# Hybrid decoder block on one core: order of the first two experts' products and of four experts' weight loads, and three small moves

## The chip, the cores and the metric

The kernel runs on one core of one Trainium2 chip. The metric is the device time of one execution in microseconds (us), as the median of several runs. The engines are TensorE (PE, with its weight loads as PEld), VectorE (DVE), ScalarE (ACT), GpSimd (POOL) and SyncE (SP), which issues nearly all DMAs.

## The reference

One layer on 256 tokens of width 1024: a mixer part (an S5 state-space branch and an attention branch with indexer-chosen keys), and then a mixture of 32 experts, 4 for each token:

```
x = x + W_out( sigmoid(g_ssm) * P_ssm(y_ssm) + sigmoid(g_att) * P_att(y_att) )
h = rms_norm(x, norm2_g)
gates = softmax over the top 4 of (h @ w_router + b_router)
for e in range(32):
    z = h @ w_moe_in[e] + b_moe_in[e]                 # 1024 -> 2048
    zg, zl = min(z[:, ::2], 7), clip(z[:, 1::2], -7, 7)
    act = zg * sigmoid(1.702 * zg) * (zl + 1)
    out += gates[:, e:e+1] * (act @ w_moe_out[e] + b_moe_out[e])   # 1024 -> 1024
x = rms_norm(x + out, norm_f_g)
```

Everything is float32. The weights of the experts are 32 times 12.6 MB and are read from HBM once.

## The kernel before

**Memory.** The tensor `mem` holds 24 slots of 1 MB (128 partitions of 2048 floats). An expert has 12: eight with the weights of its input products, four with those of its output products. Even experts live in slots 0 to 11, odd ones in 12 to 23. Two neighbouring slots are a chunk, so an expert is four input chunks (n = 0 to 3) and two output chunks (n = 4, 5). During the mixer part the slots hold the mixer's data, and experts 0 and 1 are loaded into them one after the other as they come free (`load_first`, line 333).

**The loads.** SP issues DMAs in the order of its program, and before each it waits until the chunk that it overwrites has been used: `chunk_used` counts chunks of which TensorE has finished the matmuls. So a load of expert e + 2 waits for the same chunk of expert e. `load_first_pieces` (line 400) loads expert 2 in smaller pieces, each behind a mark `first_used` that TensorE sets inside a chunk. Then come the chunks of expert 3, and after that pairs of experts up to 31. The first experts come in loads of 2 MB, the middle ones of 4 MB, the last expert's last slots in pieces.

**An expert on TensorE** (`body`, line 1474), for expert j:
- input products (line 1496): 8 slots, 8 matmul records each, into PSUM banks 0 and 1; after the first slot (the fourth for expert 0) the input bias (line 1509), and for expert 1 also the output biases of all experts (line 1514);
- `scatter(j - 1)` (line 1469): adds the previous expert's output to the token sums in banks 4 to 7;
- `gather(j + 1)` (line 1452): picks the next expert's token rows into bank 3;
- four transposes of the activation into bank 0 (line 1522), two of the gates (line 1526) into bank 1, and `gather_t(j + 1)` (line 1460), which transposes the gathered rows;
- output products (line 1536) into bank 2.

DVE clamps and multiplies the activation (lines 1104 to 1110), makes the gate matrices, and copies the gathered rows and the transposed gates (line 1115, semaphore `gated_t_ok`) out of PSUM. ACT makes the sigmoid (line 667), copies the gathered rows (`h_tok`, line 648), the transposed activation (`act_t`, line 670) and the output sums (`y_tok`, line 678, in the same place as `h_tok`). The next expert's input products wait for `h_sel_ok` and `gated_t_ok`.

**The last expert** (`last_body`, line 1543) works in two halves of columns. ACT's part of it is `halves_of_act` (line 652).

**In the mixer part** TensorE transposes the first attention probabilities (`turn_prob(0)`, line 1297) and then makes the gate projection A3 (line 1337, two column blocks m).

Of the kernel before, what the change touches and what calls it, by code (L numbers as in the profile page):

```python
# [23 lines left out]
D = 1024  # L24
# [51 lines left out]
def build(nc, io, out):  # L76
# [3 lines left out]
    with ExitStack() as ctx:  # L80
# [100 lines left out]

        def act_tile(k):

            return act_t[:, 2 * (k // 4) + k % 2, k // 2 % 2, :]

# [138 lines left out]
        def _(sp):  # L324
# [68 lines left out]
            def one_pass(c, first, most_tokens=None):  # L393
# [6 lines left out]
                def load_first_pieces():  # L400

                    def piece(n, first_col, end, arrived):
                        sp.dma_start(place_of(0, n)[:, first_col:end], expert_part(2, n)[:, first_col:end]).then_inc(
                            arrived, 16)

                    sp.wait_ge(first_used, 1)
                    piece(0, 0, SW // 2, pieces_in)
                    sp.wait_ge(first_used, 2)
                    piece(0, SW // 2, SW, pieces_in)
                    sp.wait_ge(chunk_used, 1)  # L410
                    piece(0, SW, 2 * SW, moe_in[0][0])
# [70 lines left out]
        def _(ac):  # L482
# [162 lines left out]
            def one_pass(c, first, most_tokens=None):  # L645
                def gathered_rows(j):
                    ac.wait_ge(gathered, j + 1)
                    ac.activation(h_tok, ps[:, 3, :], ACT.Copy).then_inc(h_tok_ok, 1)  # L648

                turned = ps[:, 0, :].rearrange("p (j q s) -> p j q s", q=2, s=SLOTS)  # L650

                def halves_of_act(j):

                    ac.wait_ge(first_z_gate, c + 1)
                    ac.activation(sig[:, 0:256], gate_z[:, 0:256], ACT.Sigmoid, scale=ALPHA).then_inc(first_sig_ok, 1)
                    ac.wait_ge(z_gate, j + 1)
# [7 lines left out]
                def whole_act(j):  # L664

                    ac.wait_ge(z_gate, j + 1)
                    ac.activation(sig, gate_z, ACT.Sigmoid, scale=ALPHA).then_inc(sig_ok, 1)  # L667
                    gathered_rows(j + 1)
                    ac.wait_ge(act_trans, j + 1)
                    ac.activation(act_t, turned, ACT.Copy).then_inc(act_t_ok, 1)  # L670

                def body(j, tail=False):
                    if tail:
                        halves_of_act(j)
                    else:
                        whole_act(j)
                    ac.wait_ge(chunk_used, j * NT + NT)
                    ac.activation(y_tok, ps[:, 2, :], ACT.Copy).then_inc(y_tok_ok, 1)  # L678
                gathered_rows(first)
                body(first)  # L680
                if most_tokens:
                    most_tokens()
                with ac.Fori(1, NE - 1) as e:
# [21 lines left out]
        def _(ve):  # L705
# [334 lines left out]
            def one_pass(c, first, most_tokens=None):  # L1040
# [58 lines left out]

                def body(j, e):  # L1100
                    choose(e + 1)
                    ve.wait_ge(chunk_used, j * NT + NT_IN)
                    z = ps[:, 0:2, :].rearrange("p b (c g) -> p g (b c)", g=2)
# [18 lines left out]
                if isinstance(c, int):  # L1122
                    gates_out()
                body(first, 0)
                if most_tokens:
                    most_tokens()
                with ve.Fori(1, NE - 1) as e:
                    body(e + first, e)
# [18 lines left out]
        def _(pe):  # L1147
# [298 lines left out]
            def one_pass(c, first, most_tokens=None):  # L1446
# [26 lines left out]

                def body(j, odd, pair=None, big=None, head=False, out_bias=False):

                    def arrived(n):

                        if big is None:
                            pe.wait_ge(moe_in[odd][n], pair)
                        elif n % RUN == 0:  # L1480
                            pe.wait_ge(big_in[odd][n // RUN], big)

                    def weights(k):

                        return mem[:, (12 * odd + k) * SW:(12 * odd + k + 1) * SW]

# [3 lines left out]
                    for k in range(KD):  # L1490
                        if k % CH == 0:
                            arrived(k // CH)
                        w = weights(k)
# [22 lines left out]
                    if not head:  # L1516
                        scatter(j - 1)
                    gather(j + 1)
# [4 lines left out]
                    i.then_inc(act_trans, 1)  # L1523
                    pe.wait_ge(gated_ok, j + 1)
# [3 lines left out]
                    gather_t(j + 1)  # L1528

                    pe.wait_ge(act_t_ok, j + 1)  # L1530
                    for k in range(KF):
                        if k % (2 * CH) == 0:
                            arrived(NT_IN + k // (2 * CH))
                        w = weights(KD + k // 2)[:, (k % 2) * D:(k % 2) * D + D]
                        for q in range(2):
                            i = pe.matmul(ps[64 * q:64 * q + SLOTS, 2, :], act_tile(k), w[:, 512 * q:512 * q + 512],  # L1536
                                          start=(k == 0), stop=(k == KF - 1))
                        if head and isinstance(c, int) and k == 1:
                            i.then_inc(first_used, 1)
                        if k % (2 * CH) == 2 * CH - 1:  # L1540
                            i.then_inc(chunk_used, 1)

                def last_body(j):
# [84 lines left out]
                begun = 16 * SMALL * c  # L1628
                body(first, 0, pair=begun + 16, head=True)
                body(first + 1, 1, pair=begun + 16, out_bias=isinstance(c, int))  # L1630
                if most_tokens:
                    pe.wait_ge(pieces_in, 64)
                    most_tokens()
# [155 lines left out]
```

## Time and profile before

| what | value |
|---|---|
| median of 3 runs | 1137.95 us (1137.3 to 1138.54) |
| profiled execution | 1136.45 us, of which the span is 1134.6 us |
| PE busy | 1102.4 us, 97% of the span |
| DVE busy | 342.1 us, 30% |
| ACT busy | 154.7 us, 14% |
| granted TensorE clock, mean | 0.999 |
| DMA | 437.28 MB, mean 385 GB/s |

Busy times are sums over an engine's instructions with overlaps counted once. Around the span lie 1.85 us of the profiled execution's own time. Times below count from the span's start.

### The profile page before, as it was taken

The page shows a single profiled execution, that of the slowest core. Times are in us where ns is not written, and L with a number is a line of the kernel's source. Part 1 is how long each engine was busy: PE and PEld are TensorE (multiplying, and loading weights), DVE is VectorE, ACT ScalarE, POOL GpSimd, SP SyncE. Part 2 cuts the span into 40 slices and gives each one's busy share as a digit, 9 for nine tenths or more (in the row PEclk, how much of TensorE's full clock was granted, in tenths as well). Part 3 has the DMA queues.
Part 4 walks back from the last instruction along what each step waited for, and adds up shares of the span by engine and source line. Part 5 has one row for each costly group of instructions (what it writes and reads, how often), then busy time and mean ns, then how long its engine had stood idle before and what let it go on. Part 6 is the DMA issues. An engine that isn't in the chain of part 4 may idle for free.

```text
span 1134.6 us, 13388 instructions
## 1 busy us (share of the span) xinstructions
PE 1102.4 (97%) x5570; PEld 482.9 (43%) x5570; DVE 342.1 (30%) x761; ACT 154.7 (14%) x319; POOL 0.7 (0%) x8
## 2 busy tenths in 40 slices
PE   9999999999999999999999999999999999999996
PEld 8888888833333333333333333333333333333332
DVE  7999993132121111111111111111111111111112
ACT  2410361220100000100000000000000000000002
POOL 0000000000000000000000000000000000000000
PEclk9999999999999999999999999999999999999999
DMA  8444577799999999999999999999999999999996
GB/s 341 140 151 143 197 290 313 325 362 401 427 427 436 429 435 429 430 434 430 432 434 429 432 433 431 434 431 430 434 430 432 433 430 432 433 424 427 427 425 261
DMA packets 26095, 437.28 MB, mean 385 GB/s; under 512 B 3152, under 2 KB 3408, under 8 KB 6096
## 3 DMA queue, kind: packets, MB, share of 16 engines
q1 hardware_dynamic: 25632, 436.05, 91.2%
q10 hardware_dynamic: 432, 0.79, 0.2%
q8 instruction: 23, 0.38, 0.1%
q14 instruction: 8, 0.07, 0.0%
HBM read 434.99 MB, written 1.05 MB: 384 GB/s over the span
## 4 chain that ended last, share of the span: by engine, by line
PE 63%; DMA 22%; DVE 6%; issue 1%; ACT 0%; another core or an unknown queue 0%; SPq 0%; DVEq 0%; ACTq 0%
PE ps L1496 29%; DMA mem<-in_w_moe 22%; PE ps L1536 13%; PE ps L1469 4%; PE ps L1452 4%; PE ps L1398 2%; PE ps L1509 2%; DVE mem L714 2%; PE ps L1572 1%; PE ps L1169 1%; PE ps L1356 1%; PE ps L1460 1%; PE ps L1522 1%; DVE mem L901 1%; DVE xs L714 1%
## 5 line engine op out<-in xcount | busy, mean ns | idle before, releaser
L1496 PE MATMUL ps<-mem,late 128*64 128x512 f32 x1984 | 440.9, 595 | 17.0 <-DMA mem<-in_w_moe 17.0
L1496 PEld LDWEIGHTS ps<-mem,late 128*64 128x64 f32 x1984 | 138.2, 137 | 313.6 <-issue 283.0
L1104 DVE TENSOR_SCALAR late<-ps 128x512 f32<-128x512 f32 x31 | 21.4, 692 | 658.6 <-PE ps L1496 658.6
L1536 PE MATMUL ps<-mem,late 128*64 128x512 f32 x992 | 219.7, 595 | 0.0
L1169 PE MATMUL ps<-mem 128*128 128x256 f32 x608 | 135.3, 381 | 0.2 <-issue 0.2
L1536 PEld LDWEIGHTS ps<-mem,late 128*64 128x64 f32 x992 | 68.5, 137 | 129.1 <-issue 124.1
L1169 PEld LDWEIGHTS ps<-mem 128*128 128x128 f32 x608 | 114.4, 190 | 19.2 <-issue 4.0
L667 ACT ACTIVATE late<-late 128x512 f32<-128x512 f32 x31 | 19.5, 630 | 491.0 <-DVE late L1104 491.0
L1469 PE MATMUL ps<-late 64*128 64x512 f32 x256 | 63.6, 615 | 0.9 <-ACT late L678 0.9
L1452 PE MATMUL ps<-xs,late 128*64 128x512 f32 x256 | 61.9, 604 | 0.2 <-DVE late L714 0.2
L714 DVE TENSOR_TENSOR mem<-mem 128x1024 f32<-128x1024 f32 (+8 forms) x88 | 60.0, 723 | 1.3
L678 ACT ACTIVATE late<-ps 128x512 f32<-128x512 f32 x32 | 19.1, 597 | 227.2 <-PE ps L1536 223.5
L714 DVE TENSOR_TENSOR late<-late 128x128 f32<-128x128 f32 (+3 forms) x99 | 38.5, 417 | 7.1 <-ACT late L643 1.3
L1469 PEld LDWEIGHTS ps<-late 64*128 64x128 f32 x256 | 22.1, 186 | 41.9 <-issue 41.9
L1509 PE MATMUL ps<-bias_rows,late 32*64 32x512 f32 x248 | 33.7, 613 | 0.0
L1452 PEld LDWEIGHTS ps<-xs,late 128*64 128x64 f32 x256 | 15.7, 136 | 42.2 <-issue 41.5
L714 DVE TENSOR_TENSOR late<-ps,vec 128x512 f32<-128x512 f32 x32 | 22.1, 692 | 35.5 <-PE ps L1460 35.5
L714 DVE TENSOR_TENSOR mem<-ps,mem 128x1024 f32<-128x1024 f32 (+2 forms) x30 | 25.9, 899 | 17.2 <-PE ps L1356 9.2
L648 ACT ACTIVATE late<-ps 128x512 f32<-128x512 f32 x32 | 19.2, 599 | 73.9 <-PE ps L1452 73.9
L1398 PE MATMUL ps<-mem 128*128 128x256 f32 x128 | 28.9, 380 | 0.0
L1398 PEld LDWEIGHTS ps<-mem 128*128 128x128 f32 x128 | 23.8, 190 | 3.4 <-issue 0.4
L714 DVE TENSOR_TENSOR late<-table,late 128x128 f32<-128x128 f32 x96 | 24.6, 283 | 0.2
(185 smaller groups left out, 527.0 us busy)
## 6 DMA issues: line engine op xcount, KB each, us to landing
mem<-in_w_moe SPq DMA_DIRECT2D x66, 4096.0 KB, 41.3
mem<-in_w_moe SPq DMA_DIRECT2D x54, 2048.0 KB, 16.0
mem<-in_w_mix SPq DMA_DIRECT2D x26, 1024.0 KB, 6.0
mem<-in_w_moe SPq DMA_DIRECT2D x10, 1024.0 KB, 22.8
mem<-in_w_moe SPq DMA_DIRECT2D x4, 512.0 KB, 18.0
out<-xs SPq DMA_DIRECT2D x2, 512.0 KB, 2.8
mem<-in_x_t ACTq DMA_DIRECT2D x3, 256.0 KB, 4.9
mem<-mem SPq DMA_DIRECT2D x12, 64.0 KB, 2.0
```

Source lines behind the costliest of these rows:

```text
L648: ac.activation(h_tok, ps[:, 3, :], ACT.Copy).then_inc(h_tok_ok, 1)
L667: ac.activation(sig, gate_z, ACT.Sigmoid, scale=ALPHA).then_inc(sig_ok, 1)
L678: ac.activation(y_tok, ps[:, 2, :], ACT.Copy).then_inc(y_tok_ok, 1)
L714: return ve.tensor_tensor(out_, a, b, op)
L1104: ve.tensor_scalar(gate_z, z[:, 0], LIMIT, None, ALU.min).then_inc(z_gate, 1)
L1169: i = pe.matmul(b[:, m * T:m * T + T], slot[:, k, first_m + m, :], src[:, k, :], start=(k == 0), stop=(k == kt - 1))
L1398: i = pe.matmul(b[:, 0:T], wide(f"W{m // 2}")[:, k, m % 2, :], mixed[:, k, :], start=(k == 0), stop=(k == KD - 1))
L1452: i = pe.matmul(ps[64 * q:64 * q + SLOTS, 3, :], one_hot[:, t, :], xs[:, t, 512 * q:512 * q + 512], start=(t == 0), stop=(t == TT - 1))
L1469: i = pe.matmul(ps[:, 4 + 2 * t + q, :], gated_t[r, t * P:t * P + P], y_tok[r, :], start=False, stop=False, skip_group_check=True)
L1496: i = pe.matmul(ps[r, n // 2, :], h_sel[:, k % 4, k // 4, :], w[:, 512 * n:512 * n + 512], start=(k == 0), stop=(k == KD - 1))
L1509: pe.matmul(ps[r, n // 2, :], chosen[g, n, :], b_in[g, :], start=False, stop=False)
L1536: i = pe.matmul(ps[64 * q:64 * q + SLOTS, 2, :], act_tile(k), w[:, 512 * q:512 * q + 512], start=(k == 0), stop=(k == KF - 1))
```

## The change

The first two experts are no longer two `body` calls. `first_pair` does the input products of expert 0, its activation, the input products of expert 1, then the output products of 0, and those of 1. The transposed activation of expert 0 goes to the place of `h_tok` meanwhile. The loads follow this order: input chunks of expert 2 in pieces of 1 MB (two new marks after k = 4 and k = 6), input chunks of expert 3, output chunks of expert 2, output chunks of expert 3. Apart from that, three moves: the block m = 0 of A3 stands ahead of `turn_prob(0)`; for expert 30 `scatter(29)` stands behind k = 3 of the input products; in the last expert ACT copies the first half of `act_t` ahead of the second half's sigmoid.

```diff
 SP, load_first_pieces
-                    sp.wait_ge(first_used, 3)
-                    piece(1, 0, SW, pieces_in)
-                    sp.wait_ge(chunk_used, 2)
-                    piece(1, SW, 2 * SW, moe_in[0][1])
-                    load_part(1, 0, 2)
-                    load_part(1, 0, 3)
-                    sp.wait_ge(first_used, 4)
-                    piece(NT_IN, 0, SW, pieces_in)
-                    sp.wait_ge(chunk_used, NT_IN + 1)
-                    piece(NT_IN, SW, 2 * SW, moe_in[0][NT_IN])
-                    load_part(1, 0, NT - 1)
+                    for n in range(1, NT_IN):
+                        sp.wait_ge(first_used, n + 2)
+                        piece(n, 0, SW, pieces_in)
+                        sp.wait_ge(chunk_used, n + 1)
+                        piece(n, SW, 2 * SW, moe_in[0][n])
+                    for n, (half, part) in enumerate([(1, n) for n in range(NT_IN)]
+                                                     + [(h, n) for h in range(2) for n in range(NT_IN, NT)]):
+                        sp.wait_ge(chunk_used, NT_IN + n + 1)
+                        sp.dma_start(place_of(half, part), expert_part(2 + half, part)).then_inc(moe_in[half][part], 16)
...
-                    load_pair(1, halves=range(1, 2))
 ACT, last expert
+                    ac.wait_ge(first_act_trans, c + 1)
+                    ac.activation(act_t[:, 0:2], turned[:, 0:2], ACT.Copy).then_inc(first_act_t_ok, 1)
                     ac.wait_ge(z_gate, j + 1)
                     ac.activation(sig[:, 256:512], gate_z[:, 256:512], ACT.Sigmoid, scale=ALPHA).then_inc(sig_ok, 1)
-                    ac.wait_ge(first_act_trans, c + 1)
-                    ac.activation(act_t[:, 0:2], turned[:, 0:2], ACT.Copy).then_inc(first_act_t_ok, 1)
 ACT, first pair
+                def first_pair():
+                    gate_of(0)
+                    gathered_rows(1)
+                    ac.wait_ge(h_trans, 2)
+                    turned_act(0, act_t_aside)
+                    gate_of(1)
+                    sums_out(NT + NT_IN)
+                    turned_act(1, act_t)
+                    gathered_rows(2)
+                    sums_out(2 * NT)
 DVE: body(1) stands ahead of the loop, and waits for 8 chunks used instead of 10
+                    body(1, 1, used=2 * NT_IN)
 PE, mixer part
-            pe.wait_ge(tables_in, 16)
-            turn_prob(0)
             chunk_arrived(pe, "A3")
             for m in range(2):
                 for k in range(KD):
...
+                if m == 0:
+                    pe.wait_ge(tables_in, 16)
+                    turn_prob(0)
 PE, experts
-                            if head and isinstance(c, int) and (k, n) in ((0, 1), (0, 3), (2, 3)):
+                            if head and isinstance(c, int) and (k, n) in ((0, 1), (0, 3), (2, 3), (4, 3), (6, 3)):
                                 i.then_inc(first_used, 1)
...
+                        if scatter_early and k == 3:
+                            scatter(j - 1)
...
+                def first_pair():
+                    into(0, 0, pair=16, head=True)
+                    gather(1)
+                    turn_act(0)
+                    turn_gated(0)
+                    gather_t(1)
+                    pe.wait_ge(act_t_ok, 1)
+                    into(1, 1, pair=16, out_bias=True)
+                    back(0, 0, pair=16, turned=act_t_aside)
+                    turn_act(1)
+                    scatter(0)
+                    turn_gated(1)
+                    gather(2)
+                    gather_t(2)
+                    back(1, 1, pair=16)
...
-                body(first + NE - 2, 0, pair=begun + 80)
+                body(first + NE - 2, 0, pair=begun + 80, scatter_early=True)
```

`into` is the part of `body` with the waits and the input products, `back` that with the output products.

## Rows read from the trace of the kernel before

**Rows 1.** The page, part 2: GB/s in 40 equal slices of the span.
```profile
GB/s 341 140 151 143 197 290 313 325 362 401 427 427 436 429 435 429 430 434 430 432 434 429 432 433 431 434 431 430 434 430 432 433 430 432 433 424 427 427 425 261
```
**Rows 2.** Window around the first experts: busy time of each engine, clock, DMA share, GB/s.
```profile
238.00:258.00 20.00, 18.60 (x94) 6.35 (x92) 4.67 (x11) 1.82 (x3) 0.00 (x0) 1.00 0.93 364
```
**Rows 3.** Timeline of PE at its first wait for weights.
```profile
761.37 7.09 PE L1496 MATMUL ps<-mem,late 128*64 128x512 f32 x32 [1.10 <-DMA mem<-in_w_moe]
```
**Rows 4.** 2 MB loads: last input chunk of expert 2, first and last of expert 3.
```profile
L398 SPq DMA_DIRECT2D mem<-in_w_moe x1: 328/328/328, 252.5 to 252.5; - x1
DMA to landing us min/median/max: 10.0/10.0/10.0
L398 SPq DMA_DIRECT2D mem<-in_w_moe x1: 328/328/328, 269.8 to 269.8; - x1
DMA to landing us min/median/max: 9.8/9.8/9.8
L398 SPq DMA_DIRECT2D mem<-in_w_moe x1: 328/328/328, 292.3 to 292.3; - x1
DMA to landing us min/median/max: 11.8/11.8/11.8
```
**Rows 5.** 2 MB loads issued in the mixer part behind an idle or short queue.
```profile
L337 SPq DMA_DIRECT2D mem<-in_w_moe x1: 328/328/328, 140.2 to 140.2; - x1
DMA to landing us min/median/max: 7.2/7.2/7.2
L337 SPq DMA_DIRECT2D mem<-in_w_moe x1: 328/328/328, 197.1 to 197.1; - x1
DMA to landing us min/median/max: 8.7/8.7/8.7
```
**Rows 6.** Timeline of PE and DVE, experts 0 and 1: start, us, what.
```profile
245.33 7.09 PE L1496 MATMUL ps<-mem,late 128*64 128x512 f32 x32
257.00 7.09 PE L1536 MATMUL ps<-mem,late 128*64 128x512 f32 x32
257.71 0.41 DVE L1115 COPY late<-ps 128x256 f32<-128x256 f32 x1
263.92 1.89 PE L1496 MATMUL ps<-mem,late 128*64 128x512 f32 x8
279.99 1.99 PE L1469 MATMUL ps<-late 64*128 64x512 f32 x8
285.13 7.09 PE L1536 MATMUL ps<-mem,late 128*64 128x512 f32 x32
```
**Rows 7.** Timeline of PE and DVE, experts 30 and 31, and the last weight load.
```profile
1077.65 3.65 PE L1496 MATMUL ps<-mem,late 128*64 128x512 f32 x16 [0.65 <-DMA mem<-in_w_moe]
1082.54 3.65 PE L1496 MATMUL ps<-mem,late 128*64 128x512 f32 x16 [1.24 <-DMA mem<-in_w_moe]
1091.27 7.09 PE L1536 MATMUL ps<-mem,late 128*64 128x512 f32 x32
1117.09 1.94 PE L1592 MATMUL ps<-mem,late 128*64 128x512 f32 x8 [1.25 <-ACT late L659]
1117.14 0.42 DVE L714 TENSOR_TENSOR late<-late 128x256 f32<-128x256 f32 x1
1119.54 5.37 PE L1592 MATMUL ps<-mem,late 128*64 128x512 f32 x24
L447 SPq DMA_DIRECT2D mem<-in_w_moe x1: 4241/4241/4241, 1090.5 to 1090.5; - x1
DMA to landing us min/median/max: 32.1/32.1/32.1
```
**Rows 8.** Timeline of the mixer part: the first probabilities' transposes, a later DVE eviction, the third projection job.
```profile
155.41 1.06 PE L1297 MATMUL ps<-table,xs 128*128 128x128 f32 x8 [1.40 <-DVE xs L714]
170.34 1.28 DVE L714 TENSOR_TENSOR mem<-ps,mem 128x512 f32<-128x512 f32 x2
171.25 3.72 PE L1169 MATMUL ps<-mem 128*128 128x256 f32 x16
```

More of the change, by code:

```diff
@@ L180, in build, with act_tile @@
         gates_t = cut(3776, T)
-        def act_tile(k):
-            return act_t[:, 2 * (k // 4) + k % 2, k // 2 % 2, :]
+        act_t_aside = h_tok.rearrange("p (j q s) -> p j q s", q=2, s=SLOTS)
+        def act_tile(k, src=None):
+            return (act_t if src is None else src)[:, 2 * (k // 4) + k % 2, k // 2 % 2, :]
         def early_cut(base, n):
@@ L662, in halves_of_act, with gate_of, turned_act, sums_out @@
                     ready(ACT.Sqrt)
-                def whole_act(j):
+                def gate_of(j):
                     ac.wait_ge(z_gate, j + 1)
                     ac.activation(sig, gate_z, ACT.Sigmoid, scale=ALPHA).then_inc(sig_ok, 1)
+                def turned_act(j, dst):
+                    ac.wait_ge(act_trans, j + 1)
+                    ac.activation(dst, turned, ACT.Copy).then_inc(act_t_ok, 1)
+                def sums_out(used):
+                    ac.wait_ge(chunk_used, used)
+                    ac.activation(y_tok, ps[:, 2, :], ACT.Copy).then_inc(y_tok_ok, 1)
+                def first_pair():
[8 more added lines that the diff above has]
+                    sums_out(2 * NT)
+                def whole_act(j):
+                    gate_of(j)
                     gathered_rows(j + 1)
-                    ac.wait_ge(act_trans, j + 1)
-                    ac.activation(act_t, turned, ACT.Copy).then_inc(act_t_ok, 1)
+                    turned_act(j, act_t)
                 def body(j, tail=False):
@@ L676, in body @@
                         whole_act(j)
-                    ac.wait_ge(chunk_used, j * NT + NT)
-                    ac.activation(y_tok, ps[:, 2, :], ACT.Copy).then_inc(y_tok_ok, 1)
+                    sums_out(j * NT + NT)
                 gathered_rows(first)
-                body(first)
+                if isinstance(c, int):
+                    first_pair()
+                else:
+                    body(first)
+                    body(first + 1)
                 if most_tokens:
                     most_tokens()
-                with ac.Fori(1, NE - 1) as e:
+                with ac.Fori(2, NE - 1) as e:
                     body(e + first)
@@ L1098, in last_body, with body @@
                     ve.tensor_copy(gated_t, ps[:, 1, 0:T]).then_inc(gated_t_ok, 1)
-                def body(j, e):
+                def body(j, e, used=None):
                     choose(e + 1)
-                    ve.wait_ge(chunk_used, j * NT + NT_IN)
+                    ve.wait_ge(chunk_used, j * NT + NT_IN if used is None else used)
                     z = ps[:, 0:2, :].rearrange("p b (c g) -> p g (b c)", g=2)
@@ L1124, in one_pass @@
                 body(first, 0)
+                if isinstance(c, int):
+                    body(1, 1, used=2 * NT_IN)
+                else:
+                    body(first + 1, 1)
                 if most_tokens:
                     most_tokens()
-                with ve.Fori(1, NE - 1) as e:
+                with ve.Fori(2, NE - 1) as e:
                     body(e + first, e)
@@ L1472, in scatter, with arrived, weights, into @@
                             i.then_inc((first_sum_ok, second_sum_ok)[t], 1)
[L1474 to L1485, printed above, removed]
+                def arrived(odd, n, pair, big):
+                    if big is None:
+                        pe.wait_ge(moe_in[odd][n], pair)
+                    elif n % RUN == 0:
+                        pe.wait_ge(big_in[odd][n // RUN], big)
+                def weights(odd, k):
+                    return mem[:, (12 * odd + k) * SW:(12 * odd + k + 1) * SW]
+                def into(j, odd, pair=None, big=None, head=False, out_bias=False, scatter_early=False):
                     pe.wait_ge(h_sel_ok, j + 1)
@@ L1491, in body @@
                         if k % CH == 0:
-                            arrived(k // CH)
-                        w = weights(k)
+                            arrived(odd, k // CH, pair, big)
+                        w = weights(odd, k)
                         for n in range(4):
@@ L1515, in body, with turn_act @@
                                           start=False, stop=False, skip_group_check=True)
-                    if not head:
-                        scatter(j - 1)
-                    gather(j + 1)
+                        if scatter_early and k == 3:
+                            scatter(j - 1)
+                def turn_act(j):
                     pe.wait_ge(act_ok, j + 1)
@@ L1523, in body, with turn_gated @@
                     i.then_inc(act_trans, 1)
+                def turn_gated(j):
                     pe.wait_ge(gated_ok, j + 1)
@@ L1527, in body, with back @@
                     i.then_inc(gated_trans, 1)
-                    gather_t(j + 1)
+                def back(j, odd, pair=None, big=None, turned=None):
                     pe.wait_ge(act_t_ok, j + 1)
@@ L1532, in body @@
                         if k % (2 * CH) == 0:
-                            arrived(NT_IN + k // (2 * CH))
-                        w = weights(KD + k // 2)[:, (k % 2) * D:(k % 2) * D + D]
+                            arrived(odd, NT_IN + k // (2 * CH), pair, big)
+                        w = weights(odd, KD + k // 2)[:, (k % 2) * D:(k % 2) * D + D]
                         for q in range(2):
-                            i = pe.matmul(ps[64 * q:64 * q + SLOTS, 2, :], act_tile(k), w[:, 512 * q:512 * q + 512],
+                            i = pe.matmul(ps[64 * q:64 * q + SLOTS, 2, :], act_tile(k, turned), w[:, 512 * q:512 * q + 512],
                                           start=(k == 0), stop=(k == KF - 1))
-                        if head and isinstance(c, int) and k == 1:
-                            i.then_inc(first_used, 1)
                         if k % (2 * CH) == 2 * CH - 1:
                             i.then_inc(chunk_used, 1)
+                def body(j, odd, pair=None, big=None, head=False, scatter_early=False):
+                    into(j, odd, pair, big, head, scatter_early=scatter_early)
+                    if not head and not scatter_early:
+                        scatter(j - 1)
+                    gather(j + 1)
+                    turn_act(j)
+                    turn_gated(j)
+                    gather_t(j + 1)
+                    back(j, odd, pair, big)
+                def first_pair():
[13 more added lines that the diff above has]
+                    back(1, 1, pair=16)
                 def last_body(j):
@@ L1628, in one_pass @@
                 begun = 16 * SMALL * c
-                body(first, 0, pair=begun + 16, head=True)
-                body(first + 1, 1, pair=begun + 16, out_bias=isinstance(c, int))
+                if isinstance(c, int):
+                    first_pair()
+                else:
+                    body(first, 0, pair=begun + 16, head=True)
+                    body(first + 1, 1, pair=begun + 16)
                 if most_tokens:
-                    pe.wait_ge(pieces_in, 64)
+                    pe.wait_ge(pieces_in, 80)
                     most_tokens()
```

## The prediction

> **What bounds the kernel now.** I read the page's slices first. From about a quarter of the span on, HBM delivers close to 430 GB/s in every slice, while in the slices before it delivers less [rows 1]. PE is called busy 97%, so both have to be looked at. The window of the first experts shows where the DMA stream is not yet full: 364 GB/s in the 20 us from 238 on, in which expert 2's loads begin [rows 2]. Then I looked for the place where PE first waits for weights: 761.37 [rows 3]. Until there PE is the slower reader of weights that are long in memory, but the loads behind it queue up, and from there on every expert's time is the stream's. The end is therefore set by when the stream became full, plus the bytes that remain, plus what PE does after the last weights. In the tail, PE waits twice for input chunks of expert 30, 0.65 us and 1.24 us, and from 1082.54 on it is PE's own chain, with one gap of 1.25 us behind ACT at 1117.09 [rows 7]. The last piece lands at 1090.5 + 32.1 = 1122.6; PE needs it for its last sixth of the 5.37 us from 1119.54, so at 1119.54 + 5 x 0.89 = 1124.0. PE is only 1.4 us behind it.
>
> So three sums matter: the delay of the stream when it becomes full, PE's chain from 1082.5 on, and the slack between this chain and the last pieces.
>
> **Mixer part: A3's first block ahead of the transposes.** PE stands 1.40 us at 155.41 for the probabilities [rows 8]. A3's first block fills that gap (its 16 matmul records of the kind of the projection job's 16, which take 3.72 us), so A3 ends up to 1.4 us earlier. But the third projection job, at 171.25, needs a PSUM bank that DVE empties in the first half of the 1.28 us from 170.34, so at 170.98 [rows 8], and nothing in DVE's chain to there waits for PE's new order. So only 0.2 us is left. PE is dense after that, so the expert part starts 0.2 us earlier.
>
> **The first pair on PE.** Expert 0's input products end as now, at 245.33 + 7.09 = 252.4. Gather, activation and transposes are the same instructions in the same order, and take until 257.0 [rows 6]. Nothing is gained there: PE still waits for expert 0's activation before it does anything of expert 1. Then come expert 1's input products, and these wait for more than the output products did: `gated_t_ok`, which DVE gives at 257.71 + 0.41 = 258.12 [rows 6]. ACT's copy of the activation must be over too, which now waits for `gather_t`; it ends at about the same time. They start at 257.9 with the 0.2 us taken off. They last 279.99 - 263.92 = 16.1 us, to 274.0, and expert 0's output products 6.9 us, to 280.9. The activation of expert 1 is hidden behind these. Before the second output products 285.13 - 279.99 = 5.1 us of transposes, scatter and gather remain [rows 6], and ACT's copy of the gathered rows now has nothing under it, some 0.7 us. The second output products run from about 286.8 to 293.8, where they ended at 292.1 before. PE's pair takes 1.7 us longer, which costs nothing by itself: PE has slack until 761.
>
> **The first pair in the DMA stream.** This is the term that counts. Before, a load of expert 3's first chunk was issued at 269.8 and landed 9.8 us later, at 279.6; its last landed at 292.3 + 11.8 = 304.1. From the first to the last that is five more chunks in 24.5 us, 4.9 us each: full. Between the last input chunk of expert 2 (252.5 + 10.0 = 262.5) and 279.6 lie expert 2's output weights (4 MB) and the first of these chunks (2 MB): three times 4.9 us would be 14.7, it took 17.1, so 2.4 us are lost [rows 4].
>
> After, the next thing that SP may issue behind expert 2's input chunks is expert 3's first, and it has to wait until PE has used expert 1's first chunk. That takes 269.80 - 263.92 = 5.9 us from the start of its input products, since both bias groups lie inside it [rows 4, 6]: issue at 257.9 + 5.9 = 263.8. Expert 2's input chunks are then in: the new marks let four of them be issued 1 MB at a time and close a small hole, so that they land near 261 instead of 262.5. The stream stands idle, for some 5 us between landings, where the old order had issued an output slot as soon as PE had used it (257.0 + a quarter of 7.1, 258.8). The 1 MB gained early doesn't survive this hole. A 2 MB load into an idle queue landed in 7.2 us, into a partly busy one in 8.7 [rows 5]; I take 7.2, as this queue is empty. So the first chunk lands at 271.0, and all others follow without a hole, each 4.9 us later: the issues of expert 3's input chunks are 3.4 us apart, those of expert 2's output chunks fall at 277.5 and 280.9, and those of expert 3's output chunks at 290.3 and 293.8, when they need not land before 300.4 and 305.3, 10.1 and 11.5 us later. Seven more chunks: 271.0 + 7 x 4.9 = 305.3. Before it was 304.1. **The stream becomes 1.2 us later.** The bounds: landing in 8.7 gives +2.7; input products that could start at 257.0, with no wait for the copy, give +0.1.
>
> The Trainium skill ("DMA: Bandwidth & Descriptors", "Latency and other measured facts") speaks of some 2 us of fixed cost per DMA; with 4.9 us of transfer that is an estimate of 6.9 for the restart and 0.3 less in the sum. The trace has 7.2, and that is used.
>
> **The tail.** Expert 30: the scatter moves from behind the last input slot to behind the fourth. PE has 0.65 + 1.24 = 1.9 us of waits for DMA behind that place, and the scatter takes 1.9 us, so it just fits. But behind the input products its 1.9 us covered DVE's activation chain. Expert 0, which has no scatter there, shows what remains without it: 257.00 - 252.42 = 4.6 us, against 1091.27 - 1086.19 = 5.1 us in expert 30 [rows 6, 7]. The gain is 0.5 us and not 1.9. Expert 31: ACT's first-half copy no longer waits for DVE's second half, so the output products start at 1115.9 instead of 1117.09, 1.2 us earlier. The second half's product ends at 1117.14 + 0.42 = 1117.56 [rows 7], just when PE has done the first two output slices (1.8 us). So PE's chain could be 1.7 us shorter. The pieces limit it: the last lands at 1122.6, the 1 MB piece two before it by the stream's pace 2.4 us earlier, at 1120.2. PE would want that one at 1121.4 - 1.7 = 1119.7, so 0.5 us are lost to it, and the last piece at 1124.0 - 1.2 = 1122.8, which is just in time. **The tail gives 1.2 us** (0.5 if only one of the two takes effect, 1.7 if the pieces come earlier).
>
> **Sum.** +1.2 (stream, with the 0.2 us earlier start in it) - 1.2 (tail) = 0.0. Against the profiled execution (1136.45, span 1134.6) nothing changes; the median shown is 1.5 us above that execution, and the sum moves it from 1137.95 to 1138.0. 0.2% of the time is 2.3 us, about what a measurement of this kernel can tell from no change.
>
> **Rivals.**
> 1. *The restart is dear.* The landing takes 8.7 us or more, or into a queue whose engines start apart, and the tail's pieces are late by as much, so that the tail gives only 0.5: +2.7 - 0.5 = +2.2, 1140.2, and with any further wait ahead of expert 1's input products 1141. For it: in the first window the stream got 364 GB/s although issues were there [rows 2]. Against it: the idle-queue landing of 7.2. It decides if the first landing of expert 3 is later than 272.5. Chance 0.2.
> 2. *The stream runs evener after one long hole than after several small ones.* Between 304.1 and 1122.6 it moved 336 slots of 1 MB in 818.5 us, 2.436 us each. If the small holes of before left its 16 engines apart, and a restart from idle sets them level, at the 2.428 us of 4.86 us for a chunk it would gain 336 x 0.008 = 2.7 us; with the sum 0.0 that is 1135.3. For it: the landings of before are spread over 2.4 us of losses [rows 4]. Against it: 4.9 us from the first loads on, with no change later that rows show. It decides if the last landing minus that of expert 3's last chunk is under 816.5. Chance 0.1, and 0.05 more for a hole smaller than I think with the whole 1.7 us of the tail (0.1 - 1.7, 1136.3).
> 3. *The tail's moves do nothing*, because the last pieces set the end whatever PE does: +1.2, 1139.2. Against it: the 1.4 us of slack. Chance 0.1.
>
> The forecast holds the rest, 0.55, with its own range of 1136.7 to 1139.5.
>
> **Numbers.** Faster by over 0.2% needs most of rival 2: 0.13. Slower by over 0.2% is half of rival 1 and a little unforeseen: 0.17. The range from 1135.3 (rival 2) to 1140.8 (rival 1 with its bound) leaves out no more than 2 in 10.
>
> **What would show it.** Step by step: the first transposes of the probabilities start near 157.5; the second half of expert 0's input products starts at 245.1 instead of 245.33; expert 1's input products start near 257.9; the load behind them is issued at 263.8 and lands at 271; a window from 260 to 265 shows a DMA share under 0.4; the last chunk of expert 3 lands at 305.3; PE's gap between input and output products of expert 30 is 4.6 us; there is no gap at expert 31's first output products; the last piece lands 1.2 us later than 1122.6. The prediction is wrong if the first landing of expert 3 is far from 271, or if output products of expert 31 wait for their pieces longer than 0.5 us.

## The result, and the profile after

The changed kernel takes 1141.26 us (median of 8 runs, 1139.68 to 1142.83), the kernel before 1138.01 us (8 runs). The ratio is 1.0026, with a 95% interval of 1.0017 to 1.0035: 3.0 us slower by the ratio, 3.25 by the medians. Forecast was 1138.0, with a range to 1140.8. The ratios and counts below leave out two executions in a slower state (2319.12 us of the changed kernel with the hole filled, 1279.01 us of the kernel before with a longer wait of PE).

The executed order is as the prediction followed it. The times drift away from it step by step: the first transposes of the probabilities start at 157.69 (predicted 157.5), the second half of expert 0's input products at 245.42 (245.1), expert 1's input products at 258.48 (257.9), and the load behind them is issued at 265.7 (263.8). First come the windows around the first experts. Each row has the window, its length, the busy times of PE, PEld, DVE, ACT and POOL, and then the granted clock, the DMA share and GB/s. The second window lies in the hole of the stream, and the last four lie across the start of expert 1's input products:

```profile
238.00:258.00 20.00, 17.76 (x90) 5.93 (x86) 4.57 (x11) 1.82 (x3) 0.00 (x0) 0.99 0.93 364
262.00:266.00 4.00, 4.00 (x28) 1.14 (x22) 0.00 (x0) 0.00 (x0) 0.00 (x0) 1.00 0.00 0
258.00:259.00 1.00, 0.52 (x2) 0.33 (x4) 0.42 (x2) 0.00 (x0) 0.00 (x0) 0.50 1.03 434
259.00:260.00 1.00, 1.00 (x4) 0.27 (x2) 0.00 (x0) 0.00 (x0) 0.00 (x0) 0.50 1.03 434
260.00:261.00 1.00, 1.00 (x4) 0.27 (x2) 0.00 (x0) 0.00 (x0) 0.00 (x0) 0.50 0.47 197
261.00:262.00 1.00, 1.00 (x8) 0.21 (x8) 0.00 (x0) 0.00 (x0) 0.00 (x0) 0.92 0.14 57
```

The first window is as before, 364 GB/s [rows 2]. Then the hole is there: no byte between 262 and 266. And something that the prediction didn't have: TensorE's clock is 0.50, its lower level of 1.2 GHz, while expert 1's first slot is worked on. The timeline of PE and DVE shows what came ahead of it and what it cost:

```profile
256.56 0.60 PE L1491 MATMUL ps<-table,late 128*128 128x128 f32 x4
257.81 0.41 DVE L1141 COPY late<-ps 128x256 f32<-128x256 f32 x1
258.48 3.25 PE L1527 MATMUL ps<-mem,late 128*64 128x512 f32 x8 [1.32 <-DVE late L1141]
275.82 7.04 PE L1572 MATMUL ps<-mem,late 128*64 128x512 f32 x32
289.06 7.09 PE L1572 MATMUL ps<-mem,late 128*64 128x512 f32 x32
```

PE stands 1.32 us for the copy of the transposed gates. Ahead of that it waits 1.13 us for the activation and 0.28 us for the gate matrix, as it did before the change. The first slot's eight records take 3.25 us, where the same eight took 1.89 before [rows 6]: 1.36 us more. Then the loads, each with its time to landing: expert 2's last input chunk, expert 3's first, second and last chunk, and the last weight load of the kernel:

```profile
L405 SPq DMA_DIRECT2D mem<-in_w_moe x1: 327/327/327, 252.6 to 252.6; - x1
DMA to landing us min/median/max: 10.0/10.0/10.0
L422 SPq DMA_DIRECT2D mem<-in_w_moe x1: 327/327/327, 265.7 to 265.7; - x1
DMA to landing us min/median/max: 7.2/7.2/7.2
L422 SPq DMA_DIRECT2D mem<-in_w_moe x1: 328/328/328, 269.2 to 269.2; - x1
DMA to landing us min/median/max: 10.1/10.1/10.1
L422 SPq DMA_DIRECT2D mem<-in_w_moe x1: 328/328/328, 296.2 to 296.2; - x1
DMA to landing us min/median/max: 12.4/12.4/12.4
L447 SPq DMA_DIRECT2D mem<-in_w_moe x1: 4252/4252/4252, 1094.2 to 1094.2; - x1
DMA to landing us min/median/max: 33.4/33.4/33.4
```

Expert 3's first load is issued at 265.7 and lands in 7.2 us, at 272.9; the next lands at 279.3, and the last at 308.6, where it was 304.1 [rows 4]: 4.5 us later. The last load of the kernel lands at 1127.6 instead of 1122.6 [rows 7], 5.0 us later. The profiled execution is 4.7 us longer than that of before (1141.16 against 1136.45).

Expert 2's last input chunk lands at 252.6 + 10.0 = 262.6, where the prediction had it near 261, as its new marks were to close a small hole; before it was 262.5 [rows 4]. Nothing rested on that, since the stream then stands in either case.

In the tail, again PE:

```profile
1081.29 1.99 PE L1500 MATMUL ps<-late 64*128 64x512 f32 x8
1083.21 7.30 PE L1527 MATMUL ps<-mem,late 128*64 128x512 f32 x32
1093.35 0.66 PE L1554 MATMUL ps<-table,late 128*128 128x128 f32 x4 [1.13 <-DVE late L740]
1095.31 7.09 PE L1572 MATMUL ps<-mem,late 128*64 128x512 f32 x32
1120.24 1.94 PE L1653 MATMUL ps<-mem,late 128*64 128x512 f32 x8
1125.23 3.65 PE L1653 MATMUL ps<-mem,late 128*64 128x512 f32 x16 [0.59 <-DMA mem<-in_w_moe]
```

The scatter at 1081.29 fills the waits for DMA. From the end of expert 30's input products (1083.21 + 7.30 less the 0.07 by which a record overlaps the next, 1090.44) to its output products it is 4.9 us, against 5.1 before. PE now stands 1.13 us for DVE's activation, which the scatter used to cover; the prediction had 4.6. Expert 31's output products start with no gap, and PE then waits 0.59 us for a piece. From the last landing to the end of the last output products, it is 1.3 us (1127.6 to 1128.9) instead of 2.3 (1122.6 to 1124.9): the tail gave 1.0 us.

In the mixer part A3 fills the gap, and the time comes back at the third projection job:

```profile
154.14 3.72 PE L1365 MATMUL ps<-mem 128*128 128x256 f32 x16
171.37 3.69 PE L1199 MATMUL ps<-mem 128*128 128x256 f32 x16 [1.25 <-DVE mem L740]
```

### The profile page after: what moved, and what is told of

The parts are those of the page before. It is cut to its first block, busy times and chain, and to the rows that moved or that the text cites. A ratio compares the mean times of both kernels' runs of the same rounds, so it can differ in the third digit from the quotient of the medians.

```text
span 1139.1 us, 13377 instructions
## 1 busy us (share of the span) xinstructions
PE 1104.7 (97%) x5570; PEld 483.5 (42%) x5570; DVE 342.1 (30%) x761; ACT 154.7 (14%) x319; POOL 0.7 (0%) x8
## 4 chain that ended last, share of the span: by engine, by line
PE 62%; DMA 21%; DVE 7%; issue 1%; ACT 1%; another core or an unknown queue 0%; SPq 0%; DVEq 0%; ACTq 0%
PE ps L1527 30%; DMA mem<-in_w_moe 21%; PE ps L1572 14%; PE ps L1500 4%; PE ps L1483 4%; PE ps L1429 2%; PE ps L1540 2%; DVE mem L740 2%; PE ps L1387 1%; PE ps L1491 1%; PE ps L1554 1%; DVE xs L740 1%; DVE mem L927 1%; PE ps L1199 1%; DVE mem L942 1%
## 5 line engine op out<-in xcount | busy, mean ns | idle before, releaser
L740 DVE TENSOR_TENSOR mem<-ps,mem 128x1024 f32<-128x1024 f32 (+2 forms) x30 | 25.9, 899 | 17.1 <-PE ps L1387 9.2
L1554 PEld LDWEIGHTS ps<-table,late 128*128 128x128 f32 x124 | 13.0, 140 | 27.5 <-issue 23.5
```

Of the source, the lines that this page charges most:

```text
L740: return ve.tensor_tensor(out_, a, b, op)
```

## The experiments

All are measured beside the kernel before on the same chip. The ratio is to that kernel, and differences in us are worked out from it. "Landing" is the last landing of expert 3's weights minus the first issue for expert 2, from each profile; it takes out the up to 1.2 us by which the expert part as a whole starts earlier or later in one profile than in another (first issues from 238.4 to 239.6). It is 65.7 for before and 70.1 for the changed kernel.

| kernel | median us | ratio (95% interval) | landing |
|---|---|---|---|
| three moves alone | 1136.97 | 0.9991 (0.9982 to 1.0) | 66.0 |
| first pair alone | 1142.57 | 1.0041 (1.0027 to 1.0055) | 68.8 |
| changed, 4 matmuls in the second idle stretch | 1140.95 | 1.0025 (1.0014 to 1.0036) | 69.7 |
| changed, hole filled | 1139.19 | 1.0007 (0.9997 to 1.0016) | 68.2 |
| changed, 2 + 2 matmuls in both idle stretches | 1140.41 | 1.0019 (1.0011 to 1.0028) | 68.8 |
| changed, 2 + 2 matmuls, hole filled | 1136.92 | 0.9991 (0.9982 to 0.9999) | 66.5 |
| before, PE waits longer at expert 0 | 1139.15 | 1.001 (1.0001 to 1.0019) | 67.3 |
| before, stream stopped | 1145.77 | 1.0064 (1.005 to 1.0079) | 74.1 |
| ACT's swap alone | 1136.48 | 0.9987 (0.9978 to 0.9996) | 65.8 |
| early scatter alone | 1137.94 | 0.9996 (0.9987 to 1.0005) | 66.3 |
| A3's block alone | 1138.42 | 0.9999 (0.999 to 1.0008) | 66.2 |
| three moves, fine pieces | 1136.48 | 0.9987 (0.9978 to 0.9996) | 66.2 |

**The two halves of the change.** First the three moves without the first pair, and the first pair without the three moves.

> The kernel before with the three small moves alone (A3's first block ahead of the transposes, expert 30's scatter behind k = 3, ACT's first-half copy ahead of the second sigmoid). Theory A (the moves give what was predicted, the loss is all in the first pair): 1.2 us faster than before, gap of expert 30 between input and output products 4.6 us, no gap at expert 31's first output products. Theory B (the last pieces set the end whatever PE does, so the moves give nothing): within 0.3 us of before.

> The changed kernel without the three small moves, so the order of the first pair and its loads alone. Theory A (hole in the stream of weights, and TensorE's clock that falls in the longer idle time of PE ahead of expert 1's input products): 4 to 4.5 us slower than before; expert 3's first chunk issued near 265.7, its last landing near 308.6, a stretch of half clock near 258 to 261. Theory B (moves give nothing): the same as the changed kernel, 3.2 us slower than before.

The moves alone are 1.0 us faster (0.0 to 2.0), at the edge of what the interval resolves; the pair alone is 4.7 us slower (3.1 to 6.3). So the loss is the pair's. Theory B, which gave the moves nothing, is not borne out, though this interval alone doesn't exclude it; the swap alone, below, does. In the profile of the pair alone the clock stayed at 1.00: its landing is 68.8 and not 70.1, and that execution (1140.61) was the fastest of five; the other four had a mean clock of 0.996 or 0.997 and took 1141.75 to 1143.39. The expectation of half clock in its profile was a miss that told the most: the fall of the clock comes in most executions, not in all.

**The clock.** The changed kernel's own executions part in the same way: the five with a mean clock of 0.994 to 0.997 took 1141.16 to 1142.83 us, the three with 0.998 took 1139.68 to 1140.26. A lower clock goes with some 2 us, and 1.8 us of the loss (1139.84, the middle one of the three, against 1138.01) are there without it.

In the changed kernel, four matmuls on constants stand in PE's idle time:

```diff
                     gather_t(1)
+                    pe.wait_ge(gates_t_ok, 1)
+                    for _ in range(4):
+                        pe.matmul(ps[:, 2, 0:TB_ONE], ident, table[:, 0:TB_ONE], start=True, stop=True)
                     pe.wait_ge(act_t_ok, 1)
```

> The changed kernel with four matmuls on constants (320 columns, into a bank that nothing reads) in PE's idle time behind the transposes of expert 0. If the clock falls for that idle time and this makes the load of expert 3 late: clock at 1.00 through 250 to 270, expert 1's first slot in 1.8 us instead of 3.2, the load issued at 264.3 instead of 265.7, the last landing of expert 3 near 307.2, the median 1.4 us under the changed kernel's, its spread from run to run smaller too. If the fall of the clock has another cause: no difference.

The clock stayed up in the profile (two of seven executions still had a mean of 0.997), but the four took 2.3 us and expert 1's first slot began at 259.56. What the clock gave, the matmuls took: the time is that of the changed kernel. So two of them went behind `gather(1)`, into the other idle stretch, and two stayed:

> The changed kernel with two matmuls on constants in each of PE's two idle stretches between expert 0's input products and expert 1's (behind the gather, and behind the last transposes), so that they delay nothing: each two take 1.1 us in a stretch of 1.1 to 1.3. Four behind the transposes took 2.3 us and started expert 1 1.1 us late, as much as the clock had cost. If the fall of the clock is what idle time costs on top of the hole: clock 1.00 through 250 to 270, expert 3's first load issued at 264.3 to 264.6 (with the first load of expert 2 at 238.5), median 1.0 to 1.4 us under the changed kernel's, so 1.8 to 2.2 over before. If the clock costs nothing: 3.2 over before.

```profile
254.79 1.34 PE L1593 MATMUL ps<-table 128*128 128x320 f32 x4
257.63 1.24 PE L1598 MATMUL ps<-table 128*128 128x320 f32 x4
259.11 1.94 PE L1527 MATMUL ps<-mem,late 128*64 128x512 f32 x8 [0.24 <-DVE late L1141]
```

These are PE's rows of that kernel: the eight records take 1.94 us again, and the landing is 68.8, as in the pair alone at full clock. The time is 2.2 us over before by the ratio, with the three moves in it. That is 0.8 under the changed kernel where 1.0 to 1.4 was expected, and the two intervals overlap, so this pair of runs alone doesn't show what the clock is worth. Eight of its eleven executions had a mean clock of 0.998 or 0.999; three still had 0.997.

The other way round, the kernel before with one wait more, so that PE idles longer:

```diff
                     pe.wait_ge(act_t_ok, j + 1)
+                    if head and isinstance(c, int):
+                        pe.wait_ge(gated_t_ok, 1)
```

> The kernel before, in its own order, with one wait added: expert 0's output products wait for the copy of the transposed gates, as the change makes expert 1's input products do. PE then stands 1.1 us longer at 257. If the idle time is what lets the clock fall: in some of the executions a stretch of half clock from about 257.8 on, mean clock 0.997 in these, and a time 0.5 to 2 us longer than before (issues of the loads behind it 1.1 to 2.5 us later, of which the stream's hole passes on most). If the clock falls for another reason (the input products themselves): clock 0.998 to 0.999 in all executions, and 0.5 to 1.0 us longer than before.

Its windows:

```profile
258.00:259.00 1.00, 0.01 (x1) 0.00 (x0) 0.96 (x2) 0.00 (x0) 0.00 (x0) 1.00 0.88 377
259.00:260.00 1.00, 0.83 (x2) 0.32 (x4) 0.36 (x2) 0.00 (x0) 0.00 (x0) 0.60 1.11 475
260.00:261.00 1.00, 1.00 (x6) 0.42 (x4) 0.00 (x0) 0.00 (x0) 0.00 (x0) 0.50 1.03 442
```

PE idles through 258 and the clock is low right after it, on output products and not input products. The mean clock was 0.996 or 0.997 in seven of its executions and 0.998 or 0.999 in four; that of before was 0.998 or 0.999 in all 29 of this comparison. So it is the idle time that lets the clock fall, and not the input products that follow it in the changed kernel. The Trainium skill ("TensorE: Matmul & The Clock Gate", "A second HAM failure mode: psum-queue depth-cycling") tells of another kernel in which frequent short idle times of PE between groups of matmuls make the clock swing between its levels; the trace agrees in that three short ones, of 1.13, 0.28 and 1.16 us here, are followed by a fall, a single one. The landing became 1.6 us later and the time 1.1 us longer (0.1 to 2.2). That 1.1 us is not shown to be the clock's: the seven executions with the lower mean have a median of 1138.95 us, the other four of 1139.7, and the wait itself makes the loads behind it later too.

**The hole.** The changed kernel with expert 1's biases behind k = 3, a mark behind its first slot, and expert 3's first chunk in two pieces:

```diff
-                        if k == (3 if head else 0):
+                        if k == (3 if head or out_bias else 0):
...
-                        if out_bias and k == 0:
+                        if out_bias and k == 3:
...
+                            if out_bias and (k, n) == (0, 3):
+                                i.then_inc(first_used, 1)
...
+                            sp.wait_ge(first_used, 6)
+                            sp.dma_start(place_of(1, 0)[:, 0:SW], expert_part(3, 0)[:, 0:SW]).then_inc(pieces_in, 16)
```

> The changed kernel with the hole in the stream filled as far as it can be: both bias groups of expert 1 stand behind k = 3 instead of k = 0, and expert 3's first chunk is loaded in two pieces of 1 MB, the first behind expert 1's first slot. If the hole sets the loss: first piece issued at 261.9 (with the clock low, 260.4 without), the stream idle for 1 to 2 us instead of 6, expert 3's last landing at 304 to 305 instead of 308.6, and the median 3.5 to 4.5 us under the changed kernel's. If the loss is PE's longer pair, which takes as long as before: no difference.

> The same four matmuls together with the filled hole (biases of expert 1 behind k = 3, expert 3's first chunk in two pieces). Filled hole alone: 1.3 us over before, with the clock low from 257.7 to 261.3 in its profile. With both, the first piece is issued at 260.4 to 260.6, when the stream has just run dry, and the median is 0 to 0.5 us over before. If the clock has no part in it: 1.3 over before again.

Filling the hole takes the changed kernel from 3.0 us over before to 0.8 by the ratios, a gain of 2.2 where 3.5 to 4.5 was expected. The first piece was issued at 261.9 as expected, and the low clock was in the expectation. But the last landing came at 306.8 and not at 304 to 305: two distances between landings are 6.0 us (275.3 to 281.3) and 5.9 us (300.9 to 306.8), where the others of 2 MB behind 270.4 are 4.9. With hole filled and clock kept up, it is 1.0 us under before, the same as with the three moves alone, and the mean clock was 0.998 or 0.999 in all eleven executions. The matmuls that keep the clock up are worth 1.8 us here, and the intervals of the two ratios barely touch. So hole and clock together are the whole loss of the pair, as far as intervals of 1 us either way can tell, and without them the pair is worth nothing either.

Whether a delay of the stream at this place really reaches the end was tried with the kernel before, PE's order untouched, and SP held back:

```diff
-                    sp.wait_ge(first_used, 4)
+                    sp.wait_ge(chunk_used, NT + 1)
```

> The kernel before with nothing moved on PE; only SP waits for expert 1's first used chunk before it loads expert 2's output weights, so these two chunks are issued at 269.8 instead of 259.0 to 264.1. If a delay of the stream at this place comes out whole at the end: landings of these and all later chunks 7 to 8.5 us later (last of expert 3 at 311.5 to 312.5), and the time 7 to 8.5 us longer. If later slack takes some of it up (PE doesn't wait for weights until 761): less than 4 us longer.

The window of its profile in which the stream stands:

```profile
262.00:272.00 10.00, 10.00 (x54) 3.01 (x52) 0.00 (x0) 0.60 (x1) 0.00 (x0) 1.00 0.04 11
```

and its last load of expert 3:

```profile
L398 SPq DMA_DIRECT2D mem<-in_w_moe x1: 327/327/327, 293.5 to 293.5; - x1
DMA to landing us min/median/max: 20.2/20.2/20.2
```

PE is 100% busy all through this window; only the stream stands. The last landing comes 8.4 us later, and the time is 7.3 us longer by the ratio (5.7 to 9.0). Within that interval, a delay of the stream comes out whole at the end, 850 us later.

**The three moves one by one.**

> The kernel before with ACT's swap in the last expert alone. Theory A (each tail move does its own part): expert 31's output products start without the 1.25 us gap, PE then waits for no piece, as its chain is still 0.2 us behind the last: 1.0 to 1.2 us faster than before. Theory B (the pieces set the end and PE's earlier start is lost in waits for them): under 0.4 us faster.

> The kernel before with expert 30's early scatter alone. Theory A: the gap between its input and output products is 4.6 us instead of 5.1, 0.5 us faster than before. If the whole scatter came off the path: 1.9 us faster. If the wait for the last input chunk ends later behind the moved scatter: 0.

> The kernel before with A3's first block ahead of the transposes alone. Theory A: the 1.3 us come back at the third projection job, which waits for DVE; expert part 0.2 us earlier or not at all, time within 0.3 us of before. If the gain lasted: 1.4 us faster.

ACT's swap alone gives 1.5 us (0.5 to 2.5), which holds the predicted 1.2. PE then waits 0.61 us for a piece:

```profile
1121.36 3.65 PE L1592 MATMUL ps<-mem,late 128*64 128x512 f32 x16 [0.61 <-DMA mem<-in_w_moe]
```

So part of the chain is already the pieces', which was not expected of this kernel. The scatter alone, 0.5 us (-0.6 to 1.5), and A3's block, 0.1 us, can't be told from nothing. Since PE already waits for a piece with the swap, the scatter can add nearly nothing to it; that is argued from the wait, and no run has these two moves alone. The moved block shows the same wait for DVE at the third job as in the changed kernel (1.25 us).

**A version that beats both.** The kernel before with its order of experts 0 and 1, the three moves, expert 1's biases behind k = 3, and the loads of expert 2 and of expert 3's first chunk in pieces of 1 MB. The diff shows the loop for expert 2:

```diff
+                    for n in range(1, NT):
+                        sp.wait_ge(first_used, n + 2)
+                        piece(n, 0, SW, pieces_in)
+                        sp.wait_ge(chunk_used, n + 1)
+                        piece(n, SW, 2 * SW, moe_in[0][n])
```

> What the experiments point to: the order of the kernel before on PE with the three small moves, and the loads behind it as fine as they can be: input and output chunks of expert 2 and the first of expert 3 in pieces of 1 MB, each behind its mark, the biases of expert 1 behind k = 3. The three moves alone gave 0.9. The small holes of before (issues of 249.0, 264.1 and 269.8 could be 1.7 us earlier for their first halves, the last 3.9) leave 0.5 to 1.5 us of stream. Expected 1.5 to 2.4 us faster than before, last landing of expert 3 64.5 to 65.2 us behind the first issue instead of 65.7. If the lag is of single DMA engines and not of holes: 0.9 as without the pieces.

It is 1.5 us under before (0.5 to 2.5), the same as the swap alone, and the landing is 66.2 and not 65.2 or less. The pieces bring nothing that shows: the stream's small lags of before were not holes that earlier issues can close.

## Why the prediction was wrong

**Right.** PE's idle time ahead of expert 1 is not covered but longer, and its input products wait for the copy of the gates. The stream stands idle until expert 1's first chunk is used. The load into the idle queue lands in 7.2 us. A stream delay passes whole to the end. The tail gives 1.0 us (predicted 1.2), with the early scatter worth little since DVE's chain appears in its place, and the wait for a piece is 0.59 us (predicted 0.5). A3's block comes back at the job that waits for DVE; the 0.2 us that were to be left of it are not seen, the first load is issued at 238.5 (238.4 before).

**The term that failed** is the stream's +1.2. Measured from the first issue, the last landing of expert 3 was predicted at 305.3 - 238.2 = 67.1 and is 70.1, so 4.4 over before's 65.7 where the sum had 1.4 (1.2, and the 0.2 of the earlier start). Its parts:
- "They start at 257.9", 19.7 us behind the first issue: 20.0, so 0.3 short. The copy of the gates ends at 257.81 + 0.41 = 258.22, and PE starts 0.26 us after it; the sum had nothing for that.
- "That takes 5.9 us": 7.25 (258.48 to 265.73). The 1.35 us is the clock. No step of the prediction asked whether the longer wait would cost more than its length. The kernel before was so close to it that 1.16 us of idle time more (with one wait added) or 1.32 (changed) were enough.
- "All others follow without a hole, each 4.9 us later": the first distance was 6.4 (272.9 to 279.3), and the seven took 35.7 us, not 34.3: 1.4 short. The mistake is in the reading of [rows 4]: "it took 17.1, so 2.4 us are lost" took all of these for holes that the new order would not have. But 1.5 of them is one long distance between two landings, 273.2 to 279.6, and such a distance of 6.0 to 6.6 us stands once, between 269 and 283, in the profiles of ten of the twelve experiments too, with a full hole ahead of it or none; in the other two (fine pieces, stopped stream) it is 3.9 and 3.7 for 1 MB, instead of 2.5. The sum let the new order have a gain for it. The landing at 273.2 is that of expert 2's second output chunk, and expert 3's first load was issued 3.4 us ahead of it, at 269.8 [rows 4]. The queue was not empty, and the window between the two landings shows the stream full:

```profile
L398 SPq DMA_DIRECT2D mem<-in_w_moe x1: 328/328/328, 264.1 to 264.1; - x1
DMA to landing us min/median/max: 9.1/9.1/9.1
273.20:279.60 6.40, 6.40 (x32) 2.01 (x28) 0.00 (x0) 0.00 (x0) 0.00 (x0) 1.00 1.00 421
```

With these put right, and the tail at 1.0, the sum would have been 1.2 + 0.3 + 1.35 + 1.4 - 1.0 = +3.3, against 3.0 measured. That they meet so closely is in part luck. The terms are those of the profiled execution, which is 4.7 us longer: 0.5 more comes between expert 3's last landing and the last load's (819.0 us instead of 818.5), and some 0.7 behind the end of the last output products (4.0 us later than before). And the median is over eight executions, of which three had a mean clock of 0.998. Both signs of being wrong came: the first landing of expert 3 is 1.9 us from 271, and the wait for a piece is over 0.5 us. Rival 1 named the right direction, and its sign, a first landing later than 272.5, came too (272.9), but with the wrong mechanism: the restart was not dear, 7.2 us, and it was the issue that was late. Rival 2 wanted under 816.5 us between the last two landings named, and fell.

What makes the long distance is open. The trace's list of queues for 273 to 279 in the changed kernel shows, beside 169 packets of the loads, one packet of each of two other queues (and in 279.5 to 299 none):

```profile
q1 hardware_dynamic: 169, 2.51, 98.4%
q8 instruction: 1, 0.02, 1.1%
q14 instruction: 1, 0.01, 0.3%
```

A guess is that the DMA engine that serves these falls behind, and that a landing waits for the slowest engine. It fits that more was moved in the long distance than landed: 421 GB/s for 6.4 us are 2.7 MB in the kernel before. But no run took these packets away, and a second packet of q8 speaks against it as the whole cause: one comes between 300 and 305 in all fourteen profiles, and the distance between landings there is 4.8 to 5.1 us as elsewhere, in all but one (5.9, with the hole filled). In the kernel before, between the landings at 299.2 and 304.1:

```profile
q1 hardware_dynamic: 144, 2.10, 100.8%
q8 instruction: 1, 0.02, 1.2%
```

## What to carry to other kernels

When a stream of loads is the bound, ask of each reordering which slot is the next to be freed and when. Here expert 1's first input slots took the place of expert 0's output slots as the next that the stream waited for, and the load behind them was issued at 265.7 instead of 259.0. A lag between landings of before is a loss that a new order can save only if the rows show the queue empty there; otherwise it stays in the sum. And where other waits of TensorE stand close ahead of a new one (here 1.13 and 0.28 us), ask what the matmuls behind it take at the lower clock, beside the length of the wait.

## What the runs showed of the hardware

TensorE's granted clock fell to 0.50 (1.2 GHz) for 3.4 us behind idle stretches of 1.13, 0.28 and 1.32 us that followed each other with transposes between them, and eight matmul records took 1.36 us longer for it. With identical code it does not fall in every execution: the mean clock was 0.998 in three of the changed kernel's eight, and in one of five with the pair alone. Four matmuls on constants in the idle stretches brought the same eight records back to 1.94 us in the profile, though three of eleven executions still had a lower mean clock.

A 2 MB load issued while the stream stood landed in 7.2 us, in the changed kernel at 265.7 as in the kernel before at 140.2 [rows 5]. Behind it the landings of 2 MB in the changed kernel were 4.7 to 5.0 us apart, but for the first distance of 6.4 us.
